# Attention rounds of a two-block kernel: turns through other banks and in other steps, activation table loaded behind a round's last tile, mask added to the forget sums in three rounds, squares of the outputs one step later

## The reference

```
# "f": forgetting attention
F = cumsum(log_f)                                   # log_f from a projection of 8 columns
logits = q @ k.T * scale + F[t] - F[s];  logits = -inf where s > t
o_fox = softmax(logits) @ v
# "s": stick-breaking attention
z = q @ k.T * scale;  mask = s < t
log_one_minus = where(mask, log_sigmoid(-z), 0)
after = reverse_cumsum(log_one_minus) - log_one_minus
o_sb = where(mask, exp(log_sigmoid(z) + after), 0) @ v
o = concat(rmsnorm(o_fox), rmsnorm(o_sb));  x = x + o @ w_out
```

## Time and profile before

| | |
|---|---|
| Times of three runs | 2608.57, 2609.21, 2610.64 us; median 2609.21 |
| The profiled execution: its own time, and the span of its instructions | 2611.57 us, 2609.7 us |
| PE busy | 2561.5 us, 98% |
| PEld, DVE, ACT, POOL busy | 82%, 53%, 37%, 31% |
| Mean granted clock of PE | 0.997 of full speed |
| Rounds 0 to 7 of the attention | from about 1230 to 1783 us of the span |

### The profile page before, as it was taken

One profiled execution on the slowest core, in us unless ns is written; L12 is line 12 of the kernel. 1 busy time (PEld: TensorE's weight loads), 2 busy tenths in 40 slices (PEclk: granted clock), 3 DMA queues, 4 the chain that ended last, 5 costly groups with the idle time before them and its releaser, 6 DMA issues. The chain is left out here.

```text
span 2609.7 us, 32398 instructions
## 1 busy us (share of the span) xinstructions
PE 2561.5 (98%) x12906; PEld 2134.3 (82%) x12906; DVE 1389.8 (53%) x1286; ACT 975.4 (37%) x1377; POOL 820.8 (31%) x339
## 2 busy tenths in 40 slices
PE   8999999999999999999999999999999999999999
PEld 4888888888888888887888888887888888888887
DVE  5864547766666753445736454555854314431454
ACT  3421144444353420124556555654244213321334
POOL 3755543433434345542011101143422222222230
PEclk9999999999999999999999999999999999999999
DMA  8222321212122253341111111140111111111111
GB/s 338 81 88 71 116 71 57 80 54 70 58 72 69 86 188 105 107 148 52 33 41 41 33 41 41 33 161 18 49 48 48 49 48 48 48 49 64 49 57 65
DMA packets 56551, 194.32 MB, mean 74 GB/s; under 512 B 6856, under 2 KB 10824, under 8 KB 55152
## 3 DMA queue, kind: packets, MB, share of 16 engines
q1 hardware_dynamic: 41312, 141.74, 16.4%
q10 hardware_dynamic: 15120, 50.90, 5.5%
HBM read 158.50 MB, written 29.92 MB: 72 GB/s over the span
## 5 line engine op out<-in xcount | busy, mean ns | idle before, releaser
L238 PE MATMUL G<-H_hi,w_hi 128*128 128x512 f32 x1616 | 502.3, 392 | 1.0 <-ACT silu_zB L724 0.7
L269 POOL TENSOR_TENSOR w_lo<-w_raw,w_hi 128x1024 fp32r<-128x1024 f32 x132 | 346.4, 2625 | 491.1 <-ACT w_hi L263 485.3
L238 PE MATMUL G<-H_lo,w_hi 128*128 128x512 f32 x1616 | 497.8, 389 | 0.0
L238 PE MATMUL G<-H_hi,w_lo 128*128 128x512 f32 x1616 | 497.6, 389 | 0.0
L264 POOL TENSOR_TENSOR w_hi<-w_raw,ones 128x1024 fp32r<-128x1024 f32 x75 | 198.4, 2645 | 591.2 <-PE G L238 470.8
L238 PEld LDWEIGHTS G<-H_lo,w_hi 128*128 128x128 f32 x1616 | 303.3, 188 | 63.4
L238 PEld LDWEIGHTS G<-H_hi,w_lo 128*128 128x128 f32 x1616 | 303.3, 188 | 63.3
L238 PEld LDWEIGHTS G<-H_hi,w_hi 128*128 128x128 f32 x1616 | 300.8, 188 | 64.3 <-issue 4.4
L1857 POOL TENSOR_TENSOR w_lo<-w_raw,w_hi 128x1024 fp32r<-128x1024 f32 x24 | 60.2, 2507 | 480.8 <-ACT w_hi L2073 480.8
L1964 PEld LDWEIGHTS G<-att_v,probsT 128*128 128x128 f32 x1152 | 147.9, 193 | 21.7 <-ACT probsT L2102 12.9
L1912 PE MATMUL G<-A_hi,w_hi 128*128 128x512 f32 x368 | 155.9, 424 | 7.3 <-DVE projected L2255 6.5
(11 more groups left out here) (532 smaller groups left out, 4728.1 us busy)
## 6 DMA issues: line engine op xcount, KB each, us to landing
w_raw<-w_in SPq DMA_DIRECT2D x65, 512.0 KB, 3.6
w_raw<-w_up SPq DMA_DIRECT2D x44, 512.0 KB, 3.6
pre_raw<-w_in SPq DMA_DIRECT2D x30, 512.0 KB, 3.7
wm<-w_mod SPq DMA_DIRECT2D x8, 1024.0 KB, 18.4
w_raw<-w_out SPq DMA_DIRECT2D x16, 512.0 KB, 3.7
w_raw<-w_down SPq DMA_DIRECT2D x16, 512.0 KB, 3.6
xT<-xT SPq DMA_DIRECT2D x8, 512.0 KB, 19.1
b_d<-silu_zB ACTq DMA_DIRECT2D x8, 512.0 KB, 2.6
```

The costliest lines, as they stand in the source:

```text
L238: mm = nc.tensor.matmul(dst[:, n * NB:n * NB + c], w[:, k, :], m[:, k, n * NB:n * NB + c], start=first, stop=last)
L269: nc.gpsimd.tensor_tensor(w_lo[:, slot, 0:kt, :], w_raw[:, slot, 0:kt, :], w_hi[:, slot, 0:kt, :].bitcast(F32), ALU.subtract).then_inc(w_r ...
```

## The change

It has six parts.

1. `v_turned` goes from n=0, behind `values`, to n=1, ahead of `values`; `v_copied` follows it to n=1.
2. The first half of a round's turned outputs goes into the upper bank of the second score pair (G) and no longer into a U bank, except in the last round; `scores` of tile 5 of a round waits for its copy by ACT.
3. Behind tile 15 of each round but the last, ACT runs an ACTIVATE of one column with the function that the next round uses, so that the activation table for it is loaded there.
4. In rounds 1, 3 and 5 the mask is no longer a matmul. POOL adds it: for each tile it copies the block of 128 columns that was masked last back from the forget sums and adds the mask to the next block, in a copy of the sums (`masked_sums`, which is the first `not_taken` buffer), and `first` reads that copy. In round 7 the mask stays with PE.
5. POOL's `w_lo` products stand in the same program, between these.
6. The squares of a round's outputs are made at m=3 and 4, no longer at 2 and 3.

```diff
         nots = [take("not_taken", [P, T]), fsum[1]]
+        masked_sums = nots[0]
...
         mn = take("row_mins", [P, 2, 1])
+        warm = take("table_loaded", [P, 1])
...
+        def mask_in_sums(g):
+            return tile_of(g)[0] == "f" and g // TILES < ROUNDS - 1
...
             q, n = stream(s)
-            if n == 0 and q <= ROUNDS:
+            if n == 1 and q <= ROUNDS:
...
             if s > TILES and s % TILES == 2:
-                for half in range(2):
-                    use_u(("o", 2 * (s // TILES - 1) + half), ("act", "outT", 2 * (s // TILES - 1) + half))
+                use_u(("o", 2 * (s // TILES) - 1), ("act", "outT", 2 * (s // TILES) - 1))
...
+        def bank_of_out(r, half):
+            return bank_of_u(("o", 2 * r + half)) if half or r == ROUNDS - 1 else Z[1][:, NB:T]
...
                 split(j, j % 2, j // 2 + 1)
-            for j in range(J_ATT + 2, J_OUT2 + 2):
-                S.wait(g, "act", "w high", j)
-                g.tensor_tensor(w_lo[:, j % 2], w_raw[:, j % 2], w_hi[:, j % 2].bitcast(F32), ALU.subtract).then_inc(w_ready, 1)
+            def masked(t):
+                _, hh, tt = tile_of(t)
+                S.wait(g, "dve", "first", t - 1)
+                if tt == 0:
+                    g.wait_ge(nf_landed[hh], 16 * (t // TILES // 2 + 1))
+                else:
+                    back = slice((tt - 1) * P, tt * P)
+                    g.tensor_copy(masked_sums[:, back], fsum[hh][:, back])
+                block = slice(tt * P, (tt + 1) * P)
+                S.mark("pool", "masked", g.tensor_tensor(masked_sums[:, block], fsum[hh][:, block], maskb[:, 0, :], ALU.add), t)
+            for s in range(-TILES - SHIFT, STEPS - TILES):
+                q, n = stream(s)
+                if s + 1 >= 0 and mask_in_sums(s + 1):
+                    masked(s + 1)
+                j = J_ATT + 3 * q + {1: 1, 7: 2, 12: 3}.get(n, KT * KT)
+                if J_ATT + 2 <= j <= J_OUT2 + 1:
+                    S.wait(g, "act", "w high", j)
+                    g.tensor_tensor(w_lo[:, j % 2], w_raw[:, j % 2], w_hi[:, j % 2].bitcast(F32), ALU.subtract).then_inc(w_ready, 1)
...
+            def read(g):
+                S.wait(pe, *(("dve", "first", g) if tile_of(g)[0] == "f" else ("act", "taken", g)))
...
                     S.wait(pe, "act", ("rstd12 copied", "rstd1 copied")[g], 1)
-                elif tile_of(g - 2)[0] == "f":
-                    S.wait(pe, "dve", "first", g - 2)
                 else:
-                    S.wait(pe, "act", "taken", g - 2)
+                    read(g - 2)
+                if g > TILES and g % TILES == 5:
+                    S.wait(pe, "act", "outT", 2 * (r - 1))
...
                     pe.matmul(z[:, cols], Qh[hh][:, t], Ks[hh][:, cols], start=True, stop=False)
-                    pe.matmul(z[:, cols], Ql[hh][:, t], Ks[hh][:, cols], start=False, stop=tt // 4 != b)
-                S.mark("pe", "z", pe.matmul(z[:, tt * P:w], identb, maskb[:, "fs".index(x), :], start=False, stop=True), g)
+                    mm = pe.matmul(z[:, cols], Ql[hh][:, t], Ks[hh][:, cols], start=False, stop=mask_in_sums(g) or tt // 4 != b)
+                if not mask_in_sums(g):
+                    mm = pe.matmul(z[:, tt * P:w], identb, maskb[:, "fs".index(x), :], start=False, stop=True)
+                S.mark("pe", "z", mm, g)
...
                 for half in range(2):
-                    u = U_AT["o", 2 * r + half]
-                    S.wait(pe, *U_FREE[u - 2])
+                    if ("o", 2 * r + half) in U_AT:
+                        S.wait(pe, *U_FREE[U_AT["o", 2 * r + half] - 2])
+                    else:
+                        read(TILES * (r + 1) - 1)
                     for b in range(4):
-                        mm = pe.transpose(U[u % 2][:, b * P:(b + 1) * P], ON[:, 4 * half + b, :], ident)
+                        mm = pe.transpose(bank_of_out(r, half)[:, b * P:(b + 1) * P], ON[:, 4 * half + b, :], ident)
...
                     piece(q, PIECE_AT[n][0])
+                if n == 1 and 1 <= q <= ROUNDS:
+                    v_turned(q - 1)
...
                     values(s - 1)
-                if n == 0 and 1 <= q <= ROUNDS:
-                    v_turned(q - 1)
...
                 S.wait(act, "pe", "z", g)
-                S.wait(act, "dve", "first", g - 2)
+                S.wait(act, "dve", "first", g - 2 if g % TILES else g - 1)
...
                     S.wait(act, "pe", "out turned", 2 * r + half)
-                    S.mark("act", "outT", act.activation(OT[:, half * NB:(half + 1) * NB], bank_of_u(("o", 2 * r + half)), ACT.Identity, scale=gain), 2 * r + half)
+                    S.mark("act", "outT", act.activation(OT[:, half * NB:(half + 1) * NB], bank_of_out(r, half), ACT.Identity, scale=gain), 2 * r + half)
...
                         probs(nxt)
-                if n == 0 and 1 <= q <= ROUNDS:
+                if nxt % TILES == TILES - 1 and 0 <= nxt < STEPS - 1:
+                    act.activation(warm, epsc, ACT.Exp if tile_of(nxt)[0] == "s" else ACT.Sigmoid)
+                if n == 1 and 1 <= q <= ROUNDS:
...
                         act.dma_start(fsum[1], nf_d[r:r + 1, :].to_broadcast([P, T])).then_inc(nf_landed[1], 16)
-                    if r and m in (2, 3):
+                    if r and m in (2, 3, 4):
...
                             act.dma_start(o_d[out_row(r - 1)], OT).then_inc(o_stored[out_row(r - 1)], 16)
-                        squares(r - 1, m - 2)
+                        else:
+                            squares(r - 1, m - 3)
...
                     r = g // TILES
-                    if tt == 0:
+                    if mask_in_sums(g):
+                        S.wait(v, "pool", "masked", g)
+                    elif tt == 0:
...
                     S.wait(v, "pe", "z", g)
-                    do("first", v.tensor_tensor_reduce(out=p, in0=fsum[hh][:, 0:w], in1=Z[g % 2][:, 0:w], scale=1.0, scalar=1e30,
+                    do("first", v.tensor_tensor_reduce(out=p, in0=(masked_sums if mask_in_sums(g) else fsum[hh])[:, 0:w], in1=Z[g % 2][:, 0:w], scale=1.0, scalar=1e30,
```

## The result

| | before | after |
|---|---|---|
| Median, lowest to highest, runs | 2609.20 us (2607.04 to 2611.94, 10) | 2616.22 us (2612.42 to 2619.3, 10) |
| Ratio of times, 95% interval | | 1.0025 [1.0017, 1.0034] |
| Profiled execution, its span, its clock | 2611.57, 2609.7 us, 0.997 | 2612.52, 2610.7 us, 0.995 |
| Time that the half clock cost, mean of the runs | 5.8 us (21 runs) | 16.5 us |
| Mean time less that | 2603.4 us | 2599.5 us |

The account below looks back on a forecast made before the run. PE, busy 98% of the span, bounds the kernel, with ACT setting the third evac in rounds 2, 4, 6. Terms sum to -4.6 us, four clock falls add 6.8, giving +2.2: 2611.4 us, range 2600 to 2619.

Parts of the forecast that it names:

- the forecast's main case: Waits gather at six round boundaries, with three or more falls to half clock: 2609.5 to 2615 us, chance 0.47.
- The waits gather: Rounds 1 to 6: PE's short waits become one of about 2.3 to 2.5 us at the third evac.
- The delay of `out_of`: Rounds 1, 3, 5: out_of waits for the later second four squares, so its chain starts about 0.8 us later.
- v: Seven round boundaries: the copy of v is hidden behind values of one tile, gaining 0.4 us each.
- round 0: Start of round 0: later v delays w_high, so the first long wait grows from 2.32 to 3.3 us, +1.0 us.
- tile 28: Rounds 1, 3, 5: POOL's mask comes late behind w_lo, so PE's scores of tile 30 start 0.55 us late.
- masks: Rounds 1, 3, 5: each mask matmul gone saves PE 0.13 us; nine of 16 a round count, -1.2 us each.
- table: Ahead of round 7: the earlier activation table load gains 0.7 us, besides 0.4 us for v.
- The clock: Four falls at six boundaries at 1.7 us each, +6.8 us; round 7 gets 2.6 us back.
- The rival with no fall: Waits gather at the boundaries but at most one fall to half clock follows: -4.6 us, 2604.6 us, chance 0.15.
- The rival in which the waits don't gather: ACT or DVE finds room, so PE gains what it waits for: -19.5 us, 2590 us, chance 0.2.
- The rival in which POOL decides: w_lo grows beside DVE and masks of tiles 1 and 7 come late too: +10 us, 2619 us, chance 0.18.

Follow-up runs that it names:

- part six alone: The kernel before with only the squares moved to m=3 and 4, nothing else of the change: 2617.38 us, 1.0034 of before.
- masks back: The changed kernel with all masks as matmuls on PE again and none on POOL: 2618.22 us, 1.0034 of before.
- v back: The changed kernel with the turn and copy of v at n=0 again: 2619.52 us, 1.0038 of before.
- the experiment with a busy PE: The changed kernel with 90 unused matmuls of 256 columns ahead of PE's wait for the third evac in rounds 1 to 6: 2607.69 us, 0.9997 of before.
- the second squares at step 7: The changed kernel with the second four squares at m=7, behind both q_high, and outputs waiting only for the squares they need: 2593.85 us, 0.9943 of before.
- the best version: The changed kernel with second squares at m=7, w_lo one step later on POOL and v of round 0 at n=0: 2590.09 us, 0.9926 of before.

## Why the prediction held in its mechanism and fell short in size

The time was forecast at 2611.4 and came out at 2616.2: inside the range of 2600 to 2619, on the side that had 0.28. The change was forecast to cost 2.2 us and cost 7.0. That is just above the 2616 at which the forecast's main case had its own upper end, so part of being inside is luck: the range was as wide as it was for the sake of rivals that did not come. Step by step:

**The waits gather: right.** 2.5 us were forecast for rounds 1, 3, 5 and 2.56, 2.56, 2.74 seen; 2.3 for rounds 2, 4, 6 and 2.12, 2.07, 2.11 seen. The 0.2 us at `outT` was 0.17. The delay of `out_of` was 1.23 us (1327.49 to 1328.72, with `outT` at 1318.44 and 1318.49) where 0.8 was taken: DVE waited for the last of the second four squares (1328.19 to 1328.50).

**v, round 0, tile 28, masks: near; table: wrong, and small.** No wait for att_v is left. Round 0 waits 2.76 and 0.27 us, 3.03 for the forecast 3.3. v is worth 3.3 us by the experiment (3.8 by the rests) where the sum had 2.8 - 1.0 = 1.8. Tile 30 waits 0.53 us (0.55 forecast), and with `w_lo` later these waits go. A masked step takes 0.28 + 0.42 = 0.70 us on POOL, 0.8 taken. The masks' net of 3 x (1.2 - 0.55) = 1.9 us came out at 2.0 (2.7 by the rests). The table load's 0.7 was not there (0.2): ahead of round 7 the 0.54 us at 1737.01 and v's 0.40 went, but the transposes of v now wait 0.65 us for the copied probabilities (1737.60), so 0.3 us went where 1.1 was forecast.

**The clock: the term that was mis-sized.** The sum had four falls of six at 1.7 us, +6.8, and 2.6 back in round 7: +4.2 net. The runs have +10.6. The profiled execution of after shows just the forecast, four falls of 3.4 us and none in round 7. Two things were mis-sized. A fall need not end after 3.4 us: behind these waits the traces of the experiments have 6.8 us (twice with part six alone, once with the masks back, once with v back) and 10.2 us (v back, from 1334.2), beside the 6.7 us in the earlier trace rows, which the forecast did not carry over to the six boundaries. The four traces that have the gathered wait (after, part six alone, masks back, v back) have 17 falls at 24 boundaries. So the share taken, four of six, was right; but the falls last 78.5 us together, 4.6 us each, which costs 2.3 us a fall instead of 1.7, and 9.8 us a kernel instead of 6.8. And before's own trace was above its mean: 0.997 over 2609.7 us is 7.8 us lost, its runs lose 5.8, so there was less to win back than the trace shows. What the falls of the timed runs looked like is not on record; that they are longer or more than in the one trace of after is worked out from their clocks. The rest of the kernel came out at -3.9 us where the sum without clock had -4.6 + 2.6 = -2.0, which took back a part.

**The rival with no fall (2604.6)** is excluded by the four falls in the trace of after, and what they cost is shown by the experiment with a busy PE, which filled the idle stretch and left the rest as it was. The Trainium skill speaks for it ("TensorE: Matmul & The Clock Gate", section on HAM oscillation: only gaps longer than all of these should set the clock back); the traces disagree, with falls behind waits of 2.56, 2.07 and 2.74 us here and 2.06 in an experiment.

**The rival in which the waits don't gather (2590)** fell for this kernel, and for a reason that one experiment removes: with the second squares at step 7 it is 2593.85, and 2590.09 with `w_lo` later. I had named what gathers them, ACT's list ahead of `q_high`, and took it as given; the list's order was part of the change itself.

**The rival in which POOL decides** is not seen: POOL's order cost 0.5 us in three places, and moving it (with v of round 0) brought 3.8 us on top of the better squares, 3.1 of them clock.

Left open: why a wait of 2.12 us in round 2 had no fall behind it in one trace and one of 2.15 had in another, why even one of 2.75 had none (round 5 with v back), and what ends a fall after 3.4, 6.8 or 10.2 us. No run here tells.

## What to carry to other kernels

Where PE is at 98%, add up not only the waits but also how they lie: several short ones that gather into one of over 2 us, as here, cost their sum, and then half of each stretch at half clock behind it. One profiled execution can show too little of that (13 us of 16.5 in after) or too much (7.8 of 5.8 in before); compare (1 - clock) x span over all runs. When an engine off the critical path has a dense stretch, ask of each instruction in it who needs its result and when: the second four squares stood in front of the one copy for which PE waited, and their result was needed by nobody until rows were overwritten. Here, moving that work behind the copy was worth 22.4 us, and the outputs' bank 0.7.

## What the runs showed of the chip that I had not expected

Falls of PE's clock behind waits of the same length differ in whether they come and in how long they last: none behind 2.12 us, 3.4 us behind 2.07 us, 6.8 us behind 2.14 us, 10.2 us behind 2.06 us. In rounds 1 to 7 of all twelve traces no fall stands behind a wait of 1.24 us or less. Ninety matmuls that compute nothing of use saved 8.5 us by keeping the clock up.

A wait is not the only thing that a fall can follow. Just ahead of the attention, in the trace of before, PE has no wait for 15 us and more and counts as busy, but for the last 3.8 us with 32 matmuls of one column each; a fall comes at their end (timeline of PE, stretch):

```profile
1184.87 3.91 PE L1888 MATMUL G<-ones,tiles_made 128*128 128x1 f32 x32
```
```profile
1188.07:1191.48 3.41, 3.41 (x11) 2.83 (x12) 1.86 (x6) 0.57 (x2) 0.00 (x0) 0.50 0.12 47
```

The matmuls that kept the clock up in the experiment had 256 columns. No run here changed the small ones, so that they cause this fall is not shown.

Small POOL steps stretch when DVE works beside them on pairs of tiles in SBUF. In the best version, at the mask of tile 28 in round 1, just ahead of `w_lo` (timelines of DVE and POOL):

```profile
1347.60 2.45 DVE L2307 TENSOR_TENSOR k_parts<-projected,k_parts 64x1024 fp32r<-64x1024 f32 x2
```
```profile
1347.62 1.35 POOL L1872 COPY not_taken<-forget_sums 128x128 f32<-128x128 f32 x1 [2.07 <-DVE row_mins L2322]
1348.93 1.41 POOL L1874 TENSOR_TENSOR not_taken<-forget_sums,bf_constants 128x128 f32<-128x128 f32 x1
...
1352.65 0.28 POOL L1872 COPY not_taken<-forget_sums 128x128 f32<-128x128 f32 x1
1352.90 0.42 POOL L1874 TENSOR_TENSOR not_taken<-forget_sums,bf_constants 128x128 f32<-128x128 f32 x1
```

The same two steps took 0.28 and 0.42 us a few microseconds later, a quarter of it. Of the 90 mask instructions of that trace nine took 1.2 us or more, and these are the nine that ran beside one of DVE's subtractions of two SBUF tiles (`q_low` or `k_low`); in the trace of after none ran beside one, and none was stretched. So a price of 0.7 us for a masked step holds only where DVE does something else.
